# Two-layer hybrid encoder on one core: the end of the expert stage reordered, with the output in four transfers

## The chip, the core and the metric

The kernel runs on one core of a Trainium2 chip. A core has TensorE (PE, matrix products and transposes), VectorE (DVE), ScalarE (ACT), GpSimd (POOL) and SyncE (SP, which here only issues DMAs). Engines run their own instruction streams and meet at semaphores. The metric is the device time of one execution in microseconds (us), lower is better.

## The reference

A sequence of 16 meta tokens and 256 real tokens (width 1024) passes two layers. Each layer has a mixer (three groups of token mixers between one input and one output projection) and a feed-forward part. The second layer's feed-forward part, the one that the change touches, is a mixture of 8 experts of which each token uses 2:

```python
def moe_swiglu(h, router_w, w_gate, w_up, w_down):
    ...
    for e in range(N_EXPERTS):
        out = out + combine[..., e:e + 1].astype(h.dtype) * swiglu(h, w_gate[e], w_up[e], w_down[e])
    return out
```

where `swiglu(h, g, u, d)` is `(silu(h @ g) * (h @ u)) @ d`, the gate and up matrices are 1024 x 3584 and the down matrix is 3584 x 1024. The result is added to `h`, and the meta tokens are dropped: 256 x 1024 floats (1 MB) are the output.

## The kernel before

**The expert stage.** It takes the second half of the execution. For each expert the at most 128 tokens that chose it are gathered into `xe_hi`/`xe_lo`. An expert's 3584 hidden columns are done in 7 chunks of 512; with 8 experts there are 56 chunks, numbered n = 0 to 55 (`LAST` is 55). Every product is made of three passes over a high and a low part of each factor (`three`): high by high, low by high, high by low. If more than 128 tokens chose one expert, a flag `crowd` is set and a second pass (`experts(1)`) is run; each engine reads the flag (`value_load`) and branches around that code.

**Weights.** A chunk has six units of 128 x 2048 floats (1 MB): two for gate, two for up, two for down. `moe_stream` has SP load them into six raw slots in order. ACT makes the high part of unit k (`hi(k)`, L768, tile `m_hi`), DVE the low part (`lo(k)`, L1130, tile `m_lo`), into a ring of four. `hi(k)` waits until PE has used unit k - 3 in full (`m_used >= k - RING + 1`), as both share a slot of the ring. The order of the 336 units puts the down units of chunk n behind the gate and up units of chunk n + 1. For the end this gives: units 328 to 331 are gate and up of chunk 55, 332 and 333 down of chunk 54, 334 and 335 down of chunk 55.

**A chunk on PE** (`experts` of the tensor block): `wide` makes the gate product (bank 0), then the up product (bank 1); ACT takes SiLU (`silu`, tile `eg`), DVE multiplies (`hidden`, L1660, tile `eh`). PE goes on with `tall(n - 1)`, the down product of the chunk before, into banks 3 and 4 (the two halves of the 1024 output columns), and then `turn_hidden(n)` transposes `eh` in four pieces (L2254, bank 2). ACT and DVE make `et_hi` and `et_lo` of it (`et_high` L1005, `et_low` L1664). There is one `et_hi` and one `et_lo`.

**The end of an expert.** When its last chunk's `tall` is done, ACT copies banks 3 and 4 scaled by the gate to `ye_hi` (`ye_high`, L1021, 1024 columns at once), DVE makes `ye_lo` (L1683), PE multiplies by the selection matrix to bring the rows back to their tokens (`scatter`, L2289 and L2290, eight products into four banks), and DVE adds the four banks to `acc` (`add_scattered`, L1695). Within the stage this overlaps the next expert; for the last expert nothing follows.

**The order at the end** is written out by hand. On PE: `tall(54)`, `turn_hidden(55)`, `tall(55)`, `scatter(7)`. On ACT and DVE:

```python
                et_high(pas, LAST)
                hi(pas * MOE_UNITS + MOE_UNITS - 2)
                hi(pas * MOE_UNITS + MOE_UNITS - 1)
                ye_high(pas, NEXP - 1)
...
                hidden(pas, LAST)
                et_low(pas, LAST)
                lo(pas * MOE_UNITS + MOE_UNITS - 2)
                lo(pas * MOE_UNITS + MOE_UNITS - 1)
                ye_low(pas, NEXP - 1)
```

After the four adds DVE reads `crowd`, branches, and does a small memset (L1740) that signals `moe_done`. SP waits for it and sends the whole of `acc` in one DMA (L683), waits until that has landed, and all engines meet at the end of the program (L330).

Of the kernel before, what the change touches and what calls it, by code (L numbers as in the profile page):

```python
# [23 lines left out]
P = 128  # L24
# [49 lines left out]
PAIRS = NEXP // 2  # L74
MOE_UNITS = 6 * CHUNKS * NEXP
RING = 4
UNIT = 2048
PART = UNIT // 2
SPLITS = 4
# [73 lines left out]
def tall_units(n):  # L153

    return chunk_units(n + 1) + 4 if n < CHUNKS * NEXP - 1 else MOE_UNITS - 2
# [171 lines left out]
def program(nc, a, out):  # L327

    ctx = ExitStack()
    with ctx:  # L330
        def sem(name):
            return ctx.enter_context(nc.semaphore(name))
# [143 lines left out]
        x_hi = put("x_hi", [P, 2, D], F32R)  # L476
        x_lo = put("x_lo", [P, 2, D], F32R)
        acc = put("acc", [P, 2, D])
        xe_hi = [put(f"xe_hi{i}", [P, KT, 2 * P], F32R) for i in range(2)]
        xe_lo = [put(f"xe_lo{i}", [P, KT, 2 * P], F32R) for i in range(2)]  # L480
        et_hi = put("et_hi", [P, 4, P], F32R)
# [13 lines left out]
        eh = put("eh", [P, 512])  # L495
        assert mark[0] <= sq_at + 4 * T * 4
        put, mark = region(u32_at)
        ye_hi = put("ye_hi", [P, D], F32R)
        ye_lo = put("ye_lo", [P, D], F32R)
        m_hi_at = (u_at, split_at, split_at + UNIT * 4, h_at)  # L500
# [29 lines left out]
        for l in range(DEPTH):  # L530
# [13 lines left out]
        crowd_ready, moe_done = sem("crowd_ready"), sem("moe_done")  # L544

        mat = lambda n: mats[:, n, :]
        ident = mat(M_ID)
# [79 lines left out]

        mslot = lambda k: (NU + SHIFT + k) % RAW_SLOTS
        LAST = CHUNKS * NEXP - 1


        def gather_step(n):
# [15 lines left out]
        def moe_stream(sp):  # L648

            def experts(pas):  # L650
                for u in range(MOE_UNITS):
                    k = pas * MOE_UNITS + u
                    if k < RAW_SLOTS:
                        sp.wait_ge(lo_ready, 2 * (NU + k - RAW_SLOTS + 1))
                    else:
                        sp.wait_ge(m_lo_ready, k - RAW_SLOTS + 1)
                    sp.dma_start(raw[:, mslot(k), :], a["moe_units"][u]).then_inc(raw_full[mslot(k)], 16)
            experts(0)

            sp.wait_ge(crowd_ready, 1)  # L660
            with sp.If(sp.value_load(crowd[0:1, 0:1], min_val=0, max_val=1) > 0):
                experts(1)


        @block.sync
        def _(sp):
            sp.dma_start(h[:, :, 0:META], a["meta_t"].rearrange("(k p) n -> p k n", p=P)).then_inc(h_in, 16)
            sp.dma_start(h[:, :, META:T], a["x_t"].rearrange("(k p) n -> p k n", p=P)).then_inc(h_in, 16)
            for u, (nk, width, pieces) in enumerate(units):
                if slot_before[u] is not None:  # L670
                    sp.wait_ge(lo_ready, 2 * slot_before[u] + 2)
                for l in range(DEPTH):
                    if u == out_units[l][2]:
                        sp.wait_ge(lo_ready, 2 * out_units[l][0])
                        sp.dma_start(w_uq[:, :, :], a["mla_w_uq"][l].rearrange("(k p) n -> p k n", p=P)).then_inc(mla_w_in, 16)
                        sp.dma_start(w_ukv[:, :], a["mla_w_ukv"][l]).then_inc(mla_w_in, 16)
                        ml[l][2].wait(sp, 0, "o", H * len(QUERIES[l]) - 1)
                v = raw_view(u)
                for c0, src in pieces:
                    sp.dma_start(v[:, :, c0:c0 + src.shape[2]], src).then_inc(raw_full[slot_of[u]], 16)  # L680
            moe_stream(sp)
            sp.wait_ge(moe_done, 1)
            sp.dma_start(out[0].rearrange("(t p) n -> p t n", p=P), acc[:, :, :]).then_inc(out_sent, 16)  # L683
            sp.wait_ge(out_sent, 16)


        @block.gpsimd
# [31 lines left out]
        def _(act):  # L719
# [282 lines left out]

            def et_high(pas, n):
                act.wait_ge(turned, pas * (LAST + 1) + n + 1)
                nc.scalar.activation(et_hi[:, :, :], heads(ps[:, 2, :]), ACT.Copy).then_inc(et_hi_ready, 1)  # L1005

            def xe_copy(pas, p, step, banks):
                act.wait_ge(gathered, 4 * (pas * PAIRS + p) + step + 1)
# [48 lines left out]
        def _(dve):  # L1057
# [603 lines left out]

            def et_low(pas, n):
                dve.wait_ge(et_hi_ready, pas * (LAST + 1) + n + 1)
                V.tensor_tensor(et_lo[:, :, :], heads(ps[:, 2, :]), et_hi[:, :, :].bitcast(F32),  # L1664
                                ALU.subtract).then_inc(et_ready, 1)

            def select(pas, p):
# [11 lines left out]
                V.tensor_copy(gslot[:, p % 2, :], ps[:, GATHER[0], 0:2]).then_inc(gslot_ready, 1)  # L1679

            def ye_low(pas, e):
                dve.wait_ge(ye_hi_ready, pas * NEXP + e + 1)
                V.scalar_tensor_tensor(ye_lo[:, :].rearrange("p (b n) -> p b n", b=2), ps[:, 3:5, :],  # L1683
                                       gslot[:, e // 2 % 2, e % 2:e % 2 + 1],
                                       ye_hi[:, :].bitcast(F32).rearrange("p (b n) -> p b n", b=2),
                                       ALU.mult, ALU.subtract).then_inc(ye_ready, 1)

            def add_scattered(pas, e, i):

                q = (3, 2, 0, 1)[i]  # L1690
                dve.wait_ge(scattered, pas * NEXP + e + 1)
                if pas or e:
                    dve.wait_ge(acc_added, 4 * (pas * NEXP + e))
                part = acc[:, q // 2, 512 * (q % 2):512 * (q % 2) + 512]
                V.tensor_tensor(part, part, ps[:, SCATTER[q], :], ALU.add).then_inc(acc_added, 1)  # L1695

            def experts(pas):
                select(pas, 0)
                for n in range(LAST + 1):
# [37 lines left out]
            dve.wait_ge(crowd_ready, 1)  # L1737
            with dve.If(dve.value_load(crowd[0:1, 0:1], min_val=0, max_val=1) > 0):
                experts(1)
            V.memset(cols[:, 59:60], 0.0).then_inc(moe_done, 1)  # L1740


        @block.tensor
        def _(pe):
# [472 lines left out]
            def views(k, nk):  # L2217
                return tuple(w[k % RING][:, :].rearrange("p (k n) -> p k n", k=nk) for w in (m_hi, m_lo))
# [9 lines left out]
                                     kt == 0, kt == KT - 1)  # L2228
                    last.then_inc(m_used, 1)

            def tall(pas, n):

                pe.wait_ge(et_ready, pas * (LAST + 1) + n + 1)
                c = n % CHUNKS
                for i in range(2):
                    k = pas * MOE_UNITS + tall_units(n) + i
                    pe.wait_ge(m_lo_ready, k + 1)
                    wh, wl = views(k, 2)
                    for j in range(2):
                        f = 2 * i + j  # L2240
                        for b in range(2):
                            cb = slice(512 * b, 512 * b + 512)
                            last = three(ps[:, 3 + b, :], (et_hi[:, f, :], et_lo[:, f, :]), (wh[:, j, cb], wl[:, j, cb]),
                                         c == 0 and f == 0, c == CHUNKS - 1 and f == 3)
                    last.then_inc(m_used, 1)

            def turn_hidden(pas, n):
                pe.wait_ge(eh_ready, pas * (LAST + 1) + n + 1)
# [32 lines left out]
            def scatter(pas, e):  # L2281

                pe.wait_ge(sel_t_ready, pas * PAIRS + e // 2 + 1)
                pe.wait_ge(ye_ready, pas * NEXP + e + 1)
                for t in range(2):
                    for hf in range(2):
                        o = ps[:, SCATTER[2 * t + hf], :]
                        s_t = sel_t[e // 2 % 2][:, e % 2, t, :]
                        mm(o, s_t, ye_hi[:, 512 * hf:512 * hf + 512], start=True, stop=False)  # L2289
                        i = mm(o, s_t, ye_lo[:, 512 * hf:512 * hf + 512], start=False, stop=True)  # L2290
                i.then_inc(scattered, 1)

            def experts(pas):
                if pas:
# [5 lines left out]
                for n in range(LAST + 1):  # L2300
# [60 lines left out]
```

## Time and profile before

| what | value |
|---|---|
| time, median of 3 runs | 2056.36 us (2055.69, 2056.36, 2062.05) |
| the profiled execution's own time | 2062.42 us |
| its span, first to last instruction | 2060.6 us |
| PE busy in the span | 1941.4 us (94%) |
| DVE busy | 1518.7 us (74%) |
| ACT busy | 1122.4 us (54%) |
| mean granted clock of PE | 0.955 of full |
| moved by DMA | 443.59 MB, 215 GB/s on average |

All times within the execution are counted from the span's start. A matrix product's record is longer than the distance to the next one, since products are pipelined: the distance between starts is what one costs, and the record's end is when its result is there. Busy shares are averages over stages with different limits, so the end of the program has to be read by itself.

### The profile page before, as it was taken

The page shows a single profiled execution, that of the slowest core. Times are in us where ns is not written, and L with a number is a line of the kernel's source. Part 1 is how long each engine was busy: PE and PEld are TensorE (multiplying, and loading weights), DVE is VectorE, ACT ScalarE, POOL GpSimd, SP SyncE. Part 2 cuts the span into 40 slices and gives each one's busy share as a digit, 9 for nine tenths or more (in the row PEclk, how much of TensorE's full clock was granted, in tenths as well). Part 3 has the DMA queues.
Part 4 walks back from the last instruction along what each step waited for, and adds up shares of the span by engine and source line. Part 5 has one row for each costly group of instructions (what it writes and reads, how often), then busy time and mean ns, then how long its engine had stood idle before and what let it go on. Part 6 is the DMA issues. An engine that isn't in the chain of part 4 may idle for free.

```text
span 2060.6 us, 26977 instructions
## 1 busy us (share of the span) xinstructions
PE 1941.4 (94%) x10940; PEld 1653.9 (80%) x10940; DVE 1518.7 (74%) x1877; ACT 1122.4 (54%) x1235; POOL 73.7 (4%) x67
## 2 busy tenths in 40 slices
PE   7998989889999987988999999999999999999996
PEld 6986858789998985767878888888888888888885
DVE  6757586555547757675668888988889898888884
ACT  4642242343334542423367777777777777777773
POOL 1001111000000001111000000000000000000000
PEclk9996899999999997989899999999999999999998
DMA  9500000645545500002559999999999999999992
GB/s 300 156 26 1 1 1 1 194 144 172 165 128 169 154 27 0 1 1 82 195 220 355 359 351 352 351 351 354 350 362 351 347 352 356 356 354 365 353 366 89
DMA packets 139122, 443.59 MB, mean 215 GB/s; under 512 B 14320, under 2 KB 94240, under 8 KB 95856
## 3 DMA queue, kind: packets, MB, share of 16 engines
q1 hardware_dynamic: 137968, 437.87, 58.5%
q0 software_dynamic: 1024, 3.93, 0.5%
q8 instruction: 89, 1.46, 0.3%
q14 instruction: 41, 0.34, 0.0%
HBM read 439.61 MB, written 2.16 MB: 214 GB/s over the span
## 4 chain that ended last, share of the span: by engine, by line
PE 86%; DVE 10%; issue 2%; ACT 1%; DMA 0%; POOL 0%; SPq 0%; DVEq 0%; ACTq 0%; POOLq 0%
PE ps L1751 22%; PE ps L1753 22%; PE ps L1752 22%; PE ps L2134 2%; PE ps L2119 2%; PE ps L2138 2%; DVE cacc L1173 2%; PE ps L1764 2%; DVE w_lo L1073 1%; PE ps L1913 1%; PE ps L2254 1%; PE ps L1960 1%; PE ps L2265 1%; PE ps L1996 1%; PE ps L1925 0%
## 5 line engine op out<-in xcount | busy, mean ns | idle before, releaser
L1130 DVE TENSOR_TENSOR m_lo<-raw,m_hi 128x2048 fp32r<-128x2048 f32 x336 | 768.5, 2291 | 145.4 <-ACT m_hi L768 145.4
L768 ACT ACTIVATE m_hi<-raw 128x2048 fp32r<-128x2048 f32 x336 | 644.0, 1918 | 273.2 <-PE ps L1753 273.2
L1751 PE MATMUL ps<-m_hi,xe_hi 128*128 128x512 f32 x896 | 358.5, 400 | 1.1 <-ACT xe_lo L1010 1.1
L1753 PE MATMUL ps<-m_lo,xe_hi 128*128 128x512 f32 x896 | 353.6, 395 | 0.0
L1752 PE MATMUL ps<-m_hi,xe_lo 128*128 128x512 f32 x896 | 353.6, 395 | 0.0
L1073 DVE TENSOR_TENSOR w_lo<-raw,w_hi 128x1024 fp32r<-128x1024 f32 (+1 forms) x164 | 183.5, 1156 | 123.8 <-ACT w_hi L733 123.7
L1751 PE MATMUL ps<-u_hi,w_hi 128*128 128x272 f32 x800 | 238.7, 298 | 15.5 <-DVE u_lo L1123 11.8
L1753 PE MATMUL ps<-u_lo,w_hi 128*128 128x272 f32 x800 | 234.9, 294 | 0.0
L1752 PE MATMUL ps<-u_hi,w_lo 128*128 128x272 f32 x800 | 233.8, 292 | 0.0
L733 ACT ACTIVATE w_hi<-raw 128x1024 fp32r<-128x1024 f32 (+1 forms) x164 | 159.6, 1002 | 124.5 <-PE ps L1753 124.4
L1753 PEld LDWEIGHTS ps<-m_lo,xe_hi 128*128 128x128 f32 x896 | 168.0, 187 | 41.2
L1751 PEld LDWEIGHTS ps<-m_hi,xe_hi 128*128 128x128 f32 x896 | 168.1, 188 | 39.9 <-ACT xe_lo L1010 1.3
L1752 PEld LDWEIGHTS ps<-m_hi,xe_lo 128*128 128x128 f32 x896 | 168.2, 188 | 38.4
L1751 PE MATMUL ps<-m_hi,et_hi 128*128 128x512 f32 x448 | 178.6, 399 | 4.9 <-DVE m_lo L1130 4.9
L1752 PE MATMUL ps<-m_hi,et_lo 128*128 128x512 f32 x448 | 177.9, 397 | 0.0
L1753 PE MATMUL ps<-m_lo,et_hi 128*128 128x512 f32 x448 | 177.7, 397 | 0.0
L1751 PEld LDWEIGHTS ps<-u_hi,w_hi 128*128 128x128 f32 x800 | 154.2, 193 | 20.0 <-issue 19.5
L1752 PEld LDWEIGHTS ps<-u_hi,w_lo 128*128 128x128 f32 x800 | 154.4, 193 | 0.5
L1753 PEld LDWEIGHTS ps<-u_lo,w_hi 128*128 128x128 f32 x800 | 154.0, 193 | 0.0
L1751 PEld LDWEIGHTS ps<-m_hi,et_hi 128*128 128x128 f32 x448 | 84.7, 189 | 25.0 <-issue 5.1
L1753 PEld LDWEIGHTS ps<-m_lo,et_hi 128*128 128x128 f32 x448 | 84.7, 189 | 20.9
L1752 PEld LDWEIGHTS ps<-m_hi,et_lo 128*128 128x128 f32 x448 | 84.7, 189 | 19.9
(373 smaller groups left out, 2770.4 us busy)
## 6 DMA issues: line engine op xcount, KB each, us to landing
raw<-in_moe_units SPq DMA_DIRECT2D x336, 1024.0 KB, 4.9
raw<-in_w_in SPq DMA_DIRECT2D x30, 1024.0 KB, 5.6
raw<-in_w_out SPq DMA_DIRECT2D x16, 768.0 KB, 5.4
raw<-in_ffn_w_gate SPq DMA_DIRECT2D x11, 1024.0 KB, 5.2
raw<-in_ffn_w_up SPq DMA_DIRECT2D x11, 1024.0 KB, 5.4
raw<-in_ffn_w_down SPq DMA_DIRECT2D x8, 896.0 KB, 4.8
raw<-in_ffn_w_down SPq DMA_DIRECT2D x4, 1024.0 KB, 5.2
w_uq<-in_mla_w_uq SPq DMA_DIRECT2D x2, 768.0 KB, 4.3
```

Of the source, the lines that this page charges most:

```text
L733: nc.scalar.activation(w_hi[q % SPLITS][:, 0:r.shape[1]], r, ACT.Copy).then_inc(hi_ready, 1)
L768: nc.scalar.activation(m_hi[k % RING][:, :], raw[:, slot, :], ACT.Copy).then_inc(m_hi_ready, 1)
L1073: V.tensor_tensor(w_lo[q % SPLITS][:, 0:r.shape[1]], r, w_hi[q % SPLITS][:, 0:r.shape[1]].bitcast(F32), ALU.subtract).then_inc(lo_ready, 1)
L1130: V.tensor_tensor(m_lo[k % RING][:, :], raw[:, mslot(k), :], m_hi[k % RING][:, :].bitcast(F32), ALU.subtract).then_inc(m_lo_ready, 1)
L1173: i = V.scalar_tensor_tensor(dst, src, w, dst, ALU.mult, ALU.add)
L1751: mm(o, w[0], x[0], start=first, stop=False)
L1752: mm(o, w[1], x[0], start=False, stop=False)
L1753: return mm(o, w[0], x[1], start=False, stop=last)
L1764: last = mm(ps[:, STAT_BANKS[k % 2], 0:width], mat(which)[0:r], sq[0:r, (piece[0] - 1) % 4, 0:width], start=(i == 0), stop=(i == len(rows) ...
L2119: i = mm(o, B[d]["M"][:, hh, :], B[d]["T"][:, hh, :], start=True, stop=True)
L2134: i = mm(ps[:, 2 * d + 1, hp * hh:hp * hh + hp], B[d]["X"][:, hh, :], level_cols(B[d]["TT"], n, 1 - d, hh), start=True, stop=True)
L2138: i = mm(ps[:, 2 * d + 1, H * hp + hp * hh:H * hp + hp * hh + hp], B[d]["TT"][:, hh, :], level_cols(B[d]["X"], n, d, hh), start=True, stop ...
```

## The change

Only the last chunk and the last expert are handled in another way, and the output is sent in another form.

- ACT: `hi(334)` and `hi(335)` stand ahead of `et_high(55)`. DVE: `lo(334)`, `hidden(55)`, `lo(335)`, `et_low(55)` in this order.
- PE: `tall` does one unit per call. In chunk 55 `turn_hidden(55)` stands between the two units of `tall(54)`. `et_hi`/`et_lo` of chunk 55 are tiles of their own, laid where `xe_hi[0]` was.
- `last_tall`: the same 24 products, but all of bank 3 first, with a signal `first_half`, then all of bank 4.
- `ye_high`, `ye_low` and the scatter of the last expert work on 512 columns at a time, and the two adds of a half follow its scatter.
- SP sends each quarter of `acc` (128 rows x 512 columns, 256 KB) as soon as it is added; `moe_done` and its memset are gone.
- All other chunks keep their order; `tall(n, 1)` repeats the wait on `et_ready`.

```diff
+QUARTERS = ((0, 0), (1, 0), (0, 1), (1, 1))
...
+        et_hi = [et_hi, nc.alloc_sbuf_tensor_at("et_hi_last", [P, 4, P], F32R, offset=xe_at)]
+        et_lo = [et_lo, nc.alloc_sbuf_tensor_at("et_lo_last", [P, 4, P], F32R, offset=xe_at + 4 * P * 4)]
...
-            sp.wait_ge(moe_done, 1)
-            sp.dma_start(out[0].rearrange("(t p) n -> p t n", p=P), acc[:, :, :]).then_inc(out_sent, 16)
-            sp.wait_ge(out_sent, 16)
+            for i, (t, hf) in enumerate(QUARTERS):
+                sp.wait_ge(acc_added, 4 * (NEXP - 1) + i + 1)
+                cs = slice(512 * hf, 512 * hf + 512)
+                sp.dma_start(out[0, P * t:P * t + P, cs], acc[:, t, cs]).then_inc(out_sent, 16)
+            sp.wait_ge(out_sent, 64)
...
+            def last_ye_high(pas, hf):
+                act.wait_ge(*((m_used, (pas + 1) * MOE_UNITS) if hf else (first_half, pas + 1)))
+                nc.scalar.activation(ye_hi[:, 512 * hf:512 * hf + 512], ps[:, 3 + hf, :], ACT.Copy,
+                                     scale=gslot[:, (PAIRS - 1) % 2, 1:2]).then_inc(ye_hi_ready, 1)
...
-                et_high(pas, LAST)
                 hi(pas * MOE_UNITS + MOE_UNITS - 2)
                 hi(pas * MOE_UNITS + MOE_UNITS - 1)
-                ye_high(pas, NEXP - 1)
+                et_high(pas, LAST)
+                act.wait_ge(gslot_ready, (pas + 1) * PAIRS)
+                last_ye_high(pas, 0)
+                last_ye_high(pas, 1)
...
+            def last_ye_low(pas, hf):
+                dve.wait_ge(ye_hi_ready, (pas + 1) * YE - 1 + hf)
+                cs = slice(512 * hf, 512 * hf + 512)
+                V.scalar_tensor_tensor(ye_lo[:, cs], ps[:, 3 + hf, :], gslot[:, (PAIRS - 1) % 2, 1:2], ye_hi[:, cs].bitcast(F32),
+                                       ALU.mult, ALU.subtract).then_inc(ye_ready, 1)
...
+            def add_last(pas):
+
+                dve.wait_ge(acc_added, 4 * (pas * NEXP + NEXP - 1))
+                for i, (t, hf) in enumerate(QUARTERS):
+                    dve.wait_ge(scattered, (pas + 1) * YE - 1 + i // 2)
+                    add_part(t, hf)
...
+                lo(pas * MOE_UNITS + MOE_UNITS - 2)
                 hidden(pas, LAST)
+                lo(pas * MOE_UNITS + MOE_UNITS - 1)
                 et_low(pas, LAST)
-                lo(pas * MOE_UNITS + MOE_UNITS - 2)
-                lo(pas * MOE_UNITS + MOE_UNITS - 1)
-                ye_low(pas, NEXP - 1)
-                for i in range(4):
-                    add_scattered(pas, NEXP - 1, i)
+                last_ye_low(pas, 0)
+                last_ye_low(pas, 1)
+                add_last(pas)
...
-            V.memset(cols[:, 59:60], 0.0).then_inc(moe_done, 1)
...
+            def last_tall(pas):
+
+                pe.wait_ge(et_ready, (pas + 1) * (LAST + 1))
+                k = pas * MOE_UNITS + MOE_UNITS - 2
+                pe.wait_ge(m_lo_ready, k + 2)
+                for b in range(2):
+                    cb = slice(512 * b, 512 * b + 512)
+                    for f in range(4):
+                        wh, wl = views(k + f // 2, 2)
+                        last = three(ps[:, 3 + b, :], (et_hi[1][:, f, :], et_lo[1][:, f, :]),
+                                     (wh[:, f % 2, cb], wl[:, f % 2, cb]), False, f == 3)
+                    if b == 0:
+                        last.then_inc(first_half, 1)
+                last.then_inc(m_used, 2)
...
+            def last_scatter(pas):
+
+                for hf in range(2):
+                    pe.wait_ge(ye_ready, (pas + 1) * YE - 1 + hf)
+                    cs = slice(512 * hf, 512 * hf + 512)
+                    for t in range(2):
+                        o = ps[:, SCATTER[2 * t + hf], :]
+                        s_t = sel_t[(PAIRS - 1) % 2][:, 1, t, :]
+                        mm(o, s_t, ye_hi[:, cs], start=True, stop=False)
+                        i = mm(o, s_t, ye_lo[:, cs], start=False, stop=True)
+                    i.then_inc(scattered, 1)
...
                     if n:
-                        tall(pas, n - 1)
+                        tall(pas, n - 1, 0)
+                    if n and n < LAST:
+                        tall(pas, n - 1, 1)
                     turn_hidden(pas, n)
-                tall(pas, LAST)
-                scatter(pas, NEXP - 1)
+                tall(pas, LAST - 1, 1)
+                last_tall(pas)
+                last_scatter(pas)
```

## Rows read from the trace of the kernel before

**Rows 1.** The page: its span, and the chain that ended last, by engine.
```profile
span 2060.6 us, 26977 instructions
...
PE 86%; DVE 10%; issue 2%; ACT 1%; DMA 0%; POOL 0%; SPq 0%; DVEq 0%; ACTq 0%; POOLq 0%
```

**Rows 2.** Stretch: length, PE, PEld, DVE, ACT, POOL busy (count), clock, DMA share, GB/s.
```profile
1997.00:2015.00 18.00, 18.00 (x81) 14.45 (x80) 15.26 (x9) 12.80 (x9) 0.00 (x0) 1.00 0.97 368
```

**Rows 3.** Timeline of PE, last full chunk: start us, us, engine, line, operation.
```profile
2023.81 0.39 PE L1753 MATMUL ps<-m_lo,xe_hi 128*128 128x512 f32 x1
...
2026.61 0.39 PE L1753 MATMUL ps<-m_lo,xe_hi 128*128 128x512 f32 x1
2026.84 0.39 PE L1751 MATMUL ps<-m_hi,et_hi 128*128 128x512 f32 x1
...
2032.44 0.60 PE L2254 MATMUL ps<-mats,eh 128*128 128x128 f32 x4
```

**Rows 4.** Timeline of ACT, the end; in brackets idle time before and its releaser.
```profile
2018.70 1.92 ACT L768 ACTIVATE m_hi<-raw 128x2048 fp32r<-128x2048 f32 x1 [0.84 <-PE ps L1753]
...
2023.32 0.57 ACT L1001 ACTIVATE eg<-ps 128x512 f32<-128x512 f32 x1
2033.07 0.60 ACT L1005 ACTIVATE et_hi<-ps 128x512 fp32r<-128x512 f32 x1 [9.18 <-PE ps L2254]
2033.57 3.70 ACT L768 ACTIVATE m_hi<-raw 128x2048 fp32r<-128x2048 f32 x2
2046.13 1.11 ACT L1021 ACTIVATE ye_hi<-ps,gslot 128x1024 fp32r<-128x1024 f32 x1 [8.86 <-PE ps L1753]
```

**Rows 5.** Timeline of DVE, the end.
```profile
2027.09 0.69 DVE L1660 TENSOR_TENSOR eh<-eg,ps 128x512 f32<-128x512 f32 x1 [1.36 <-PE ps L1753]
2033.70 0.69 DVE L1664 TENSOR_TENSOR et_lo<-ps,et_hi 128x512 fp32r<-128x512 f32 x1 [5.92 <-ACT et_hi L1005]
2035.50 4.49 DVE L1130 TENSOR_TENSOR m_lo<-raw,m_hi 128x2048 fp32r<-128x2048 f32 x2 [1.11 <-ACT m_hi L768]
2047.27 1.28 DVE L1683 SCALAR_TENSOR_TENSOR ye_lo<-ps,gslot,ye_hi 128x1024 fp32r<-128x1024 f32 x1 [7.28 <-ACT ye_hi L1021]
2051.53 2.48 DVE L1695 TENSOR_TENSOR acc<-acc,ps 128x512 f32<-128x512 f32 x4 [2.97 <-PE ps L2290]
2055.86 0.06 DVE L1740 MEMSET cols<- 128x1 f32 x1 [1.84 <-issue]
```

**Rows 6.** Timeline of PE, the last chunk's down product and the scatter.
```profile
2037.94 0.77 PE L1751 MATMUL ps<-m_hi,et_hi 128*128 128x512 f32 x1 [4.90 <-DVE m_lo L1130]
...
2045.69 0.40 PE L1753 MATMUL ps<-m_lo,et_hi 128*128 128x512 f32 x1
...
2048.70 0.47 PE L2289 MATMUL ps<-ye_hi,sel_t 128*128 128x512 f32 x1 [2.61 <-DVE ye_lo L1683]
...
2050.86 0.63 PE L2290 MATMUL ps<-ye_lo,sel_t 128*128 128x512 f32 x1
```

**Rows 7.** Busy time and granted clock in short stretches (columns as in rows 2).
```profile
2036.00:2037.00 1.00, 0.00 (x0) 0.00 (x0) 1.00 (x1) 1.00 (x1) 0.00 (x0) 0.60 0.00 0
...
2043.00:2044.00 1.00, 1.00 (x5) 0.83 (x5) 0.00 (x0) 0.00 (x0) 0.00 (x0) 0.98 0.00 0
...
2049.80:2050.20 0.40, 0.40 (x3) 0.29 (x2) 0.00 (x0) 0.00 (x0) 0.00 (x0) 0.57 0.08 21
```

**Rows 8.** DVE's instructions of the line that branches on `crowd`: duration ns, start.
```profile
L1738 DVEq COMPARE_BRANCH  x1: 72/72/72, 2052.8 to 2052.8; - x1
```

**Rows 9.** DMA issues: out<-in, queue, count, KB each, median us from issue to landing.
```profile
raw<-in_moe_units SPq DMA_DIRECT2D x336, 1024.0 KB, 4.9
...
out_h<-acc SPq DMA_DIRECT2D x1, 1024.0 KB, 4.3
...
h<-in_meta_t SPq DMA_DIRECT2D x1, 64.0 KB, 2.5
```

**Rows 10.** Timeline of SP, its last issue.
```profile
2055.94 0.40 SPq L683 DMA_DIRECT2D out_h<-acc  x1
```

More of the change, by code:

```diff
@@ L478, in program @@
         acc = put("acc", [P, 2, D])
+        xe_at = mark[0]
         xe_hi = [put(f"xe_hi{i}", [P, KT, 2 * P], F32R) for i in range(2)]
@@ L543, in program @@
             "ye_hi_ready", "ye_ready", "scattered", "acc_added"))
-        crowd_ready, moe_done = sem("crowd_ready"), sem("moe_done")
+        first_half = sem("first_half")
+        crowd_ready = sem("crowd_ready")
         mat = lambda n: mats[:, n, :]
@@ L629, in program @@
         LAST = CHUNKS * NEXP - 1
+        YE = NEXP + 1
         def gather_step(n):
@@ L662, in moe_stream @@
                 experts(1)
+                sp.wait_ge(acc_added, 8 * NEXP)
         @block.sync
@@ L1004, in et_high @@
                 act.wait_ge(turned, pas * (LAST + 1) + n + 1)
-                nc.scalar.activation(et_hi[:, :, :], heads(ps[:, 2, :]), ACT.Copy).then_inc(et_hi_ready, 1)
+                nc.scalar.activation(et_hi[n == LAST][:, :, :], heads(ps[:, 2, :]), ACT.Copy).then_inc(et_hi_ready, 1)
             def xe_copy(pas, p, step, banks):
@@ L1663, in et_low @@
                 dve.wait_ge(et_hi_ready, pas * (LAST + 1) + n + 1)
-                V.tensor_tensor(et_lo[:, :, :], heads(ps[:, 2, :]), et_hi[:, :, :].bitcast(F32),
+                V.tensor_tensor(et_lo[n == LAST][:, :, :], heads(ps[:, 2, :]), et_hi[n == LAST][:, :, :].bitcast(F32),
                                 ALU.subtract).then_inc(et_ready, 1)
@@ L1681, in ye_low @@
             def ye_low(pas, e):
-                dve.wait_ge(ye_hi_ready, pas * NEXP + e + 1)
+                dve.wait_ge(ye_hi_ready, pas * YE + e + 1)
                 V.scalar_tensor_tensor(ye_lo[:, :].rearrange("p (b n) -> p b n", b=2), ps[:, 3:5, :],
@@ L1686, in ye_low, with add_part @@
                                        ALU.mult, ALU.subtract).then_inc(ye_ready, 1)
+            def last_ye_low(pas, hf):
[3 more added lines that the diff above has]
+                                       ALU.mult, ALU.subtract).then_inc(ye_ready, 1)
+            def add_part(t, hf):
+                part = acc[:, t, 512 * hf:512 * hf + 512]
+                V.tensor_tensor(part, part, ps[:, SCATTER[2 * t + hf], :], ALU.add).then_inc(acc_added, 1)
             def add_scattered(pas, e, i):
-                q = (3, 2, 0, 1)[i]
-                dve.wait_ge(scattered, pas * NEXP + e + 1)
+                dve.wait_ge(scattered, pas * YE + e + 1)
                 if pas or e:
                     dve.wait_ge(acc_added, 4 * (pas * NEXP + e))
-                part = acc[:, q // 2, 512 * (q % 2):512 * (q % 2) + 512]
-                V.tensor_tensor(part, part, ps[:, SCATTER[q], :], ALU.add).then_inc(acc_added, 1)
+                add_part(*((1, 1), (1, 0), (0, 0), (0, 1))[i])
+            def add_last(pas):
[3 more added lines that the diff above has]
+                    add_part(t, hf)
             def experts(pas):
@@ L2229, in wide, with tall @@
                     last.then_inc(m_used, 1)
-            def tall(pas, n):
+            def tall(pas, n, i):
                 pe.wait_ge(et_ready, pas * (LAST + 1) + n + 1)
                 c = n % CHUNKS
[L2235 to L2245, printed above, removed]
+                k = pas * MOE_UNITS + tall_units(n) + i
+                pe.wait_ge(m_lo_ready, k + 1)
+                wh, wl = views(k, 2)
+                for j in range(2):
+                    f = 2 * i + j
+                    for b in range(2):
+                        cb = slice(512 * b, 512 * b + 512)
+                        last = three(ps[:, 3 + b, :], (et_hi[0][:, f, :], et_lo[0][:, f, :]), (wh[:, j, cb], wl[:, j, cb]),
+                                     c == 0 and f == 0, c == CHUNKS - 1 and f == 3)
+                last.then_inc(m_used, 1)
+            def last_tall(pas):
+                pe.wait_ge(et_ready, (pas + 1) * (LAST + 1))
+                k = pas * MOE_UNITS + MOE_UNITS - 2
+                pe.wait_ge(m_lo_ready, k + 2)
+                for b in range(2):
+                    cb = slice(512 * b, 512 * b + 512)
+                    for f in range(4):
[5 more added lines that the diff above has]
+                last.then_inc(m_used, 2)
             def turn_hidden(pas, n):
@@ L2283, in scatter @@
                 pe.wait_ge(sel_t_ready, pas * PAIRS + e // 2 + 1)
-                pe.wait_ge(ye_ready, pas * NEXP + e + 1)
+                pe.wait_ge(ye_ready, pas * YE + e + 1)
                 for t in range(2):
```

## Prediction

> **What bounds the kernel now.** The chain that ended last lies on PE for 86% of the span [rows 1], and within the expert stage on nothing else: in a stretch of 18 us near its end PE is busy for all of it at full clock, DVE 15.26 us, ACT 12.80 us [rows 2]. DMA has a share of 0.97 there, but SP is held back by raw slots that DVE frees, so the stream follows PE. A chunk is 72 products at 0.233 us (the twelve from the start at 2023.81 to that at 2026.61 took 2.80 us [rows 3]) and four transposes, 17.2 us. The change leaves that as it is. What it edits begins at 2032.4, so I read the timelines from there on as a list of who waits.
>
> PE ends `tall(54)`, transposes `eh` at 2032.44 [rows 3], and then has nothing: ACT makes `et_hi` at 2033.07 and only then `m_hi` of units 334 and 335 (3.70 us) [rows 4], DVE `et_lo` and then both `m_lo`, from 2035.50 for 4.49 us [rows 5]. PE starts on the first of them at 2037.94, idle for 4.90 us [rows 6]. In that gap its granted clock falls from 1.00 to half (mean 0.60 in the slice where it falls), and it is back only at 2043.0 [rows 7], so that the 24 products of the last `tall` take 8.16 us (2037.94 to the record end at 2046.10) instead of 5.8. Then the end of an expert runs bare: `ye_hi` 1.11 us, `ye_lo` 1.28, eight products from 2048.70 to 2051.49, the last ones again at half clock [rows 4 to 7], four adds of 2.48 us ending at 2054.01, DVE's branch and the memset at 2055.86 [rows 5], the issue at 2055.94 [rows 10], the landing 4.3 us later [rows 9], and 0.36 us to the end.
>
> **The early splits.** `hi(334)` needs unit 330 used. ACT and DVE start 0.5 us behind the start of the product that they wait for (`eh` at 2027.09 for 2026.61 [rows 3, 5]), so it starts at 2023.81 + 0.50 = 2024.3; ACT is free by then, its last work being SiLU at 2023.32 for 0.57 us. At 1.92 us [rows 4] it ends at 2026.2. `hi(335)` starts at 2026.61 + 0.50 = 2027.1 and ends at 2029.0. Both units have landed long before. The load of 335 waits for the low part of unit 329, three units ahead of the `hi(332)` at 2018.70, so `hi(329)` is at about 2018.7 - 3 x 2.8 - 0.4 = 2009.9 (with the four transposes between), its low part done 4.2 us later at 2014.1, and the load landed 4.9 us after that [rows 4, 9], at about 2019, an estimate. DVE: `lo(334)` 2026.2 to 2028.5. `hidden(55)` now stands behind it and starts at 2028.5 instead of 2027.09; what waits for it is only `turn_hidden(55)`. It ends at 2029.15. `lo(335)` 2029.1 to 2031.4.
>
> **PE.** `tall(54, 0)` runs 2026.84 to 2029.64 (12 x 0.2333). `eh` is there with 0.49 us to spare, the thinnest margin of the change; each us beyond it would be a us of PE. Transposes to 2030.1, `tall(54, 1)` to 2032.89. Under it ACT makes `et_hi` (record end of the transposes 2030.24, 0.60 us, to 2030.9) and DVE `et_lo` behind `lo(335)`, 2031.3 to 2032.0: 0.9 us to spare. The second price of an early `et_hi` would be the one tile still read by `tall(54, 1)`; the tiles of its own remove it. So `last_tall` starts at 2032.89 without a gap. There has been no idle time for the clock to fall in, and 24 products at 0.233 us end at 2038.65, its last start being 2038.26 and a record 0.39 us. Against 2046.10 that is **7.45 us** less: 5.05 of wait, 2.4 of clock.
>
> **The last expert.** Bank 3 is complete at 2035.85; its `ye_hi`, `ye_lo` hide under the other bank's 2.8 us. On the path stands the second half alone. A half `ye_hi` is costed by `et_hi`, the same engine and 512 columns (0.60, against 1.11 + 0.02 gap; saves **0.53**); a half `ye_lo` by `et_lo` (0.69 against 1.28; saves **0.59**). Scatter products of the first half fill PE from 2038.5 to 2039.4, under the split of the second. The second half's four start 0.13 us behind `ye_lo` as before, at 2040.1, and end at 2041.3 at full clock: 1.18 us against 2.81, **1.63** less. DVE adds the first half as soon as it is through with `ye_lo` (2039.9, two at 0.60 us apart), done by the time the second comes. Then two adds take 1.28 us instead of 2.48, **1.20** less, and end at 2042.6. SP waits on the adds themselves, so from 2054.01 to 2055.94, 1.93 us, only 0.03 remain: **1.90** less. The sum so far is 13.3 us: the last issue at 2042.6.
>
> **The output.** The last transfer has 256 KB. The trace has 4.3 us for 1 MB and 2.5 us for 64 KB [rows 9]; on the line between them 256 KB take 2.5 + 1.8 x 192/960 = 2.9 us, an estimate. The bounds are 2.5 and 4.3. I take 2.9, **1.4** less. The four issues are 0.6 to 0.7 us apart or more, and an issue is 0.40 us [rows 10], so SP keeps up. Landing 2045.5, end about 2045.9.
> The Trainium skill, "DMA: Bandwidth & Descriptors", section "Anatomy of one DMA", gives about 2.0 us plus bytes over 436 GB/s for GpSimd's path. For 1 MB that is an estimated 4.4 us, and this trace agrees with 4.3 for SP's. For 256 KB it is 2.6, which would make the sum 0.3 us larger.
>
> **A floor below it.** After its last add DVE still branches, and the jump past the second pass takes from 2052.8 to 2055.86 [rows 5, 8], 4.35 us counted from the end of the last scatter product. Nobody waits for it but the end of the program: 2041.3 + 4.35 = 2045.65, just what the landing gives. So a quicker landing would gain nothing, and the other cover is thin too: the end is at 2045.9 to 2046.1.
>
> **Sum.** 13.3 + 1.4 = 14.7, less 0.1 for that tie: span 2060.6 - 14.6 = 2046.0. The profiled execution took 2062.42 us, 6.06 more than the median of the runs, so the forecast is made from the median: 2056.36 - 14.6 = 2041.8 us, 0.7% less. The clock's share (2.4 here and 0.8 in the scatter) is the part that may differ among executions; all have the 4.90 us gap before.
>
> **The rivals.**
> *A, as above,* with its own range: landing at 4.3 instead of 2.9 (1.3 less gain), margins missed by half a us each, clock at half in the last four products (4 x 0.19 = 0.8): gain 12 to 15, so 2041 to 2044.5 before the spread of runs.
> *B, the clock falls nevertheless,* within `last_tall`, for instance since it falls late (in the scatter it fell at 2049.8, while PE was busy again for a us [rows 7]). A product then costs 0.427 instead of 0.233: 28 x 0.194 = 5.4 us back, 2047.2. Against it: where PE has no gap the clock is 1.00 [rows 2], and `last_tall` follows such a stretch without one.
> *C, four transfers cost more than one.* If they ran one behind another at 4.3 us each from the first issue at 2040.6, the last would land at 2057.8: gain 2.4, 2054.0, no change to be seen. Against it: the weights' units take 4.9 us each to land [rows 9] and come every 2.9 us, so transfers overlap. The milder form is the landing's bound in A.
> The Trainium skill, same page, section "Bandwidth", says to batch DMAs to 1 MB or more. As far as that concerns throughput it has no object in 1 MB of output; whether it hurts is C.
> *D, the stall stays.* One of the chains in front of `last_tall` is late (ACT or DVE held by an order that I misread) and PE idles as before, with its clock. Then 7.45 us are lost of the gain: 7.2 remain, 2049.2, at the edge of what can be told.
> *E, slower.* `tall(n, 1)` waits once more on `et_ready` in chunks 0 to 53, on the engine that bounds the stage. The gain is used up at 14.6/54 = 0.27 us each, more than a product; from 0.39 us on it is slower by 0.3% (2063). Against it: between 2026.61 and 2026.84, where PE passes the waits on `et_ready` and `m_lo_ready`, products are 0.23 us apart as elsewhere [rows 3], so a satisfied wait costs nothing visible.
>
> **Numbers.** A 0.76, B 0.06, C 0.05 (with a mild form that still gains), D 0.06, E 0.03, and 0.04 for shifts of the first thousand us that have nothing to do with this. About 0.3% (6.2 us) is what a measurement of this kernel tells from no change; the three runs of before lie 6.4 us apart. Faster: A and B, most of C's mild form, half of D: 0.92. Same 0.05, slower 0.03. The range takes A with the spread of a median upward (the runs scatter 0.7 down and 5.7 up) and B: 2039.0 to 2047.5.
>
> **What would show it.** Right: no idle time of PE between 2024 and 2038.5; the last transposes at about 2029.6, with products of `tall(54)` before and behind them; granted clock 1.00 until 2038; `m_hi` x2 before `et_hi` on ACT; `eh` at 2028.5; last add ending at 2042.6; last output issue there and landing in 2.5 to 3.2 us. Wrong: an idle gap in front of the transposes (margin 0.49 gone), a clock below 1.00 in `last_tall`, chunks longer than 17.24 us, or an end set by DVE's jump well past the landing.

## The result and the profile after

The changed kernel takes 2046.61 us (median of 6 runs, 2043.37 to 2047.77) beside 2057.12 us of the kernel before (6 runs, 2055.11 to 2062.05). The ratio is 0.9936, 95% interval 0.9923 to 0.9949: by it the kernel is 13.2 us faster, 10.5 to 15.8, while the two medians alone lie 10.5 us apart. Forecast were a gain of 14.6 us and a time of 2041.8 us. The time is 4.8 us above the forecast and within its range of 2039.0 to 2047.5; the gain forecast is within the interval.

The profiled execution has a span of 2046.0 us, the very number of the forecast, and that is luck: the change brought 0.95 us less than the sum said, and the part ahead of it happened to be 0.95 us shorter. Everything ahead of the change ran 0.95 us earlier in this execution than in the one of before: the first product of `tall(54)` starts at 2025.89 instead of 2026.84. From here on all tails are counted from that product to the end of the span: 33.76 us before, 20.11 after, a gain of **13.65 us** where the sum said 14.6.

ACT after the change, timeline of the end (columns as in rows 4; lines have moved):

```profile
2026.15 1.92 ACT L777 ACTIVATE m_hi<-raw 128x2048 fp32r<-128x2048 f32 x1 [0.88 <-PE ps L1783]
2029.33 0.60 ACT L1014 ACTIVATE et_hi_last<-ps 128x512 fp32r<-128x512 f32 x1 [1.26 <-PE ps L2298]
...
2037.73 0.69 ACT L1035 ACTIVATE ye_hi<-ps,gslot 128x512 fp32r<-128x512 f32 x1 [2.05 <-PE ps L1783]
```

DVE, the same:

```profile
2027.51 0.68 DVE L1676 TENSOR_TENSOR eh<-eg,ps 128x512 f32<-128x512 f32 x1
2028.11 2.29 DVE L1146 TENSOR_TENSOR m_lo<-raw,m_hi 128x2048 fp32r<-128x2048 f32 x1
2030.31 0.68 DVE L1680 TENSOR_TENSOR et_lo_last<-ps,et_hi_last 128x512 fp32r<-128x512 f32 x1
...
2038.45 0.75 DVE L1707 SCALAR_TENSOR_TENSOR ye_lo<-ps,gslot,ye_hi 128x512 fp32r<-128x512 f32 x1 [1.99 <-ACT ye_hi L1035]
2039.12 2.64 DVE L1712 TENSOR_TENSOR acc<-acc,ps 128x512 f32<-128x512 f32 x4
```

PE, the same (the transposes, the first product behind them, the first and last of `last_tall`, the second half's scatter):

```profile
2025.89 0.39 PE L1781 MATMUL ps<-m_hi,et_hi 128*128 128x512 f32 x1
...
2028.69 0.60 PE L2298 MATMUL ps<-mats,eh 128*128 128x128 f32 x4
2029.05 0.48 PE L1781 MATMUL ps<-m_hi,et_hi 128*128 128x512 f32 x1
...
2031.93 0.39 PE L1781 MATMUL ps<-m_hi,et_hi_last 128*128 128x512 f32 x1
...
2037.30 0.40 PE L1783 MATMUL ps<-m_lo,et_hi_last 128*128 128x512 f32 x1
...
2039.26 0.50 PE L2345 MATMUL ps<-ye_hi,sel_t 128*128 128x512 f32 x1 [0.63 <-DVE ye_lo L1707]
```

The low part of unit 335 is made by 2030.4 instead of 2040.0 [rows 5]. The transposes stand 2.80 us behind the first product of `tall(54)`, with no idle time before them. PE then goes through to the end of `last_tall` with nothing in brackets, at full clock, as two stretches of it show (columns as in rows 2):

```profile
2034.00:2036.00 2.00, 2.00 (x10) 1.59 (x9) 0.29 (x1) 0.69 (x1) 0.00 (x0) 1.00 0.00 0
2036.00:2038.00 2.00, 2.00 (x11) 1.59 (x9) 0.46 (x1) 0.27 (x1) 0.00 (x0) 1.00 0.00 0
```

The one surprise stands at the output. SP's first and last issue, each from its own stretch of the timeline, the landing times of the four, and the last instructions of DVE and SP (ns min/median/max, start):

```profile
2039.83 0.35 SPq L692 DMA_DIRECT2D out_h<-acc  x1
```
```profile
2041.79 1.47 SPq L692 DMA_DIRECT2D out_h<-acc  x1
```
```profile
DMA to landing us min/median/max: 2.2/3.1/3.8
```
```profile
L331 DVEq DRAIN  x1: 58/58/58, 2044.8 to 2044.8; - x1
...
L331 SPq DRAIN  x1: 7/7/7, 2045.8 to 2045.8; - x1
```

The last issue starts 0.03 us behind the last add, as forecast, but takes 1.47 us where the first takes 0.35, and its data land 3.8 us later. DVE is through with its jump at 2044.8, before SP.

The jumps themselves, PE's and then DVE's branch on the flag (ns min/median/max, start):

```profile
L2395 PEldq COMPARE_BRANCH  x1: 4010/4010/4010, 2040.2 to 2040.2; - x1
```
```profile
L1769 DVEq COMPARE_BRANCH  x1: 72/72/72, 2041.7 to 2041.7; - x1
```

PE's branch is under way for 4.01 us, from 2040.22 to 2044.23, and so during the last three issues. DVE's record is short, but its next instruction comes 3.1 us behind it.

### The profile page after: what moved, and what is told of

Read it like the earlier page. It is cut to its first block, busy times and chain, and to the rows that moved or that the text cites. A ratio compares the mean times of both kernels' runs of the same rounds, so it can differ in the third digit from the quotient of the medians.

```text
span 2046.0 us, 27032 instructions
## 1 busy us (share of the span) xinstructions
PE 1941.8 (95%) x10940; PEld 1654.7 (81%) x10940; DVE 1516.8 (74%) x1877; ACT 1122.4 (55%) x1236; POOL 73.9 (4%) x67
## 3 DMA queue, kind: packets, MB, share of 16 engines
q8 instruction: 90, 1.47, 0.3%
## 4 chain that ended last, share of the span: by engine, by line
PE 87%; DVE 9%; issue 1%; DMA 1%; ACT 1%; POOL 0%; DVEq 0%; POOLq 0%; ACTq 0%
PE ps L1781 22%; PE ps L1783 22%; PE ps L1782 22%; PE ps L2164 2%; PE ps L2149 2%; PE ps L2168 2%; PE ps L1794 2%; DVE cacc L1189 2%; DVE w_lo L1089 1%; PE ps L1943 1%; PE ps L2298 1%; PE ps L1990 1%; PE ps L2309 1%; PE ps L1806 1%; PE ps L2026 1%
## 5 line engine op out<-in xcount | busy, mean ns | idle before, releaser
L1781 PE MATMUL ps<-m_hi,et_hi 128*128 128x512 f32 x440 | 174.4, 396 | 0.0
L1782 PE MATMUL ps<-m_hi,et_lo 128*128 128x512 f32 x440 | 173.8, 395 | 0.0
```

The lines of the kernel that those rows point to most:

```text
L1781: mm(o, w[0], x[0], start=first, stop=False)
L1782: mm(o, w[1], x[0], start=False, stop=False)
```

## The experiments

**Late splits.** Is the largest term, 7.45 us, a wait and a clock that fell in it?

```diff
-                hi(pas * MOE_UNITS + MOE_UNITS - 2)
-                hi(pas * MOE_UNITS + MOE_UNITS - 1)
                 et_high(pas, LAST)
+                hi(pas * MOE_UNITS + MOE_UNITS - 2)
+                hi(pas * MOE_UNITS + MOE_UNITS - 1)
...
-                lo(pas * MOE_UNITS + MOE_UNITS - 2)
                 hidden(pas, LAST)
-                lo(pas * MOE_UNITS + MOE_UNITS - 1)
                 et_low(pas, LAST)
+                lo(pas * MOE_UNITS + MOE_UNITS - 2)
+                lo(pas * MOE_UNITS + MOE_UNITS - 1)
```

> The changed kernel with the split order of before on ACT and DVE (et_high(55) first, hidden and et_low(55) first, then units 334 and 335); all else as changed. All tails are measured from the first product of tall(54) to the end of the span: 33.8 us before, 20.1 us after. Theory (the 7.45 us were a wait and a clock that fell in it): PE idles some 4.5 us in front of last_tall, the granted clock falls to half in the gap, and some 10 to 12 products cost 0.43 us, 2.0 to 2.4 us in all: tail 27 us. Rival (the wait alone mattered, the clock would have been the same): 24.6 us. Rival (the early splits were not what took the wait away): 20.1 us.

Measured: tail 27.05 us. Timed against the kernel before the ratio is 0.9961 (0.9946 to 0.9975): all parts but the early splits are worth 0.4%, about 8 us of a time near 2060 (5 to 11), beside 6.7 us by the tails. PE before the last chunk's products, and the clock ahead of them and over the first twelve of them:

```profile
2036.96 0.76 PE L1781 MATMUL ps<-m_hi,et_hi_last 128*128 128x512 f32 x1 [4.31 <-DVE m_lo L1146]
```
```profile
2034.00:2035.00 1.00, 0.00 (x0) 0.00 (x0) 1.00 (x2) 0.08 (x1) 0.00 (x0) 1.00 0.00 0
```
```profile
2036.96:2042.10 5.14, 5.14 (x12) 4.08 (x13) 0.00 (x0) 0.00 (x0) 0.00 (x0) 0.50 0.01 3
```

The wait is back, and twelve products at half clock take 5.14 us. The clock fell within the gap: its mean is 0.82 from 2035.5 to 2036 and 0.50 from there on. Both parts are as expected; the second rival (early splits without effect) is out.

**Late splits, filled.** The same, with PE kept busy in the wait.

```diff
                 tall(pas, LAST - 1, 1)
+                for _ in range(18):
+                    mm(ps[:, 0, :], x_hi[:, 0, 0:P], x_lo[:, 0, 0:512], start=True, stop=True)
                 last_tall(pas)
```

> As the run with late splits, with 18 products of 512 columns (one low part by one high part of the tokens, results unused) put on PE between tall(54) and last_tall, to keep PE busy in the wait. If idleness lets the clock fall, the clock stays at 1.00, last_tall's 24 products take 5.8 us, and the tail is 24.6 us, 2.0 to 2.4 us below the unfilled one. If the clock falls for another reason, 27 us as without.

Measured: tail 24.56 us, 2.49 below the unfilled one; the clock over the last chunk's products stays full:

```profile
2035.80:2041.70 5.90, 5.85 (x25) 4.81 (x26) 0.75 (x1) 0.69 (x1) 0.00 (x0) 1.00 0.00 0
```

So the two parts of the first term come apart: 24.56 - 20.11 = 4.45 us of wait and 2.49 us of clock, which fell because PE was idle. Useless work in the gap gave a third of the term back. The two add up to 6.94 us and not to 7.45, since the gap of these kernels is 4.31 us and that of the kernel before was 4.90 [rows 6]. All further kernels were timed once, so from here on the tails of the traces are compared, not the times.

**Whole last expert.** What are the halves worth?

```diff
                 for f in range(4):
                     wh, wl = views(k + f // 2, 2)
                     for b in range(2):
...
-                last_ye_high(pas, 0)
-                last_ye_high(pas, 1)
+                act.wait_ge(m_used, (pas + 1) * MOE_UNITS)
+                nc.scalar.activation(ye_hi[:, :].rearrange("p (b n) -> p b n", b=2), ps[:, 3:5, :], ACT.Copy,
+                                     scale=gslot[:, (PAIRS - 1) % 2, 1:2]).then_inc(ye_hi_ready, 2)
```

(and `ye_low` and the scatter likewise.)

> The changed kernel without the halves: last_tall goes through both banks per 128 rows as tall does, the last ye_hi and ye_lo are 1024 columns at once, the scatter is eight products with one signal, and the four adds follow; early splits and four output transfers stay. From the profile of the changed kernel the halves were worth 0.42 (ye_hi), 0.62 (ye_lo), 1.61 (scatter) and 1.20 (adds), 3.85 us: tail 24.0 us. If the clock also falls while PE waits 2.6 us for ye_lo, 0.8 us more, 24.8 us. Rival (the halves gain nothing, since the end is set by DVE's jump past the second pass or by the output): 20 to 21 us.

Measured: tail 23.70 us, 3.59 above the changed kernel's. The clock did not fall in the wait for `ye_lo`, though it is longer; the second row is the stretch of the eight products (columns as in rows 2):

```profile
2041.07 0.50 PE L2347 MATMUL ps<-ye_hi,sel_t 128*128 128x512 f32 x1 [2.67 <-DVE ye_lo L1765]
```
```profile
2041.07:2043.19 2.12, 2.11 (x8) 1.42 (x8) 0.00 (x0) 0.00 (x0) 0.00 (x0) 1.00 0.05 12
```

The eight products take 2.12 us, against 2.79 in the kernel before, when the clock fell within them. So 3.85 us was too much for the halves by themselves: its 1.61 us for the scatter held that fall. The last issue begins 19.20 us into the tail, against 15.90 in the changed kernel: up to there the halves are worth 3.30 us. The other 0.3 us are the output's, whose issues and landings in this run are (durations in ns, then us to landing):

```profile
L692 SPq DMA_DIRECT2D out_h<-acc x4: 332/338/351, 2044.0 to 2045.8; - x4
```
```profile
DMA to landing us min/median/max: 2.4/2.7/4.1
```

All four issues are short, against 1.47 us for the changed kernel's fourth, at the same distance of 0.6 us and with the same three transfers under way. That speaks against a limit on transfers under way. But the fourth lands 4.1 us after its issue, later than any quarter of the changed kernel, so a late landing does not need a slow issue.

**One, two, three transfers, and two queues.** Where did the output's gain go? The four forms differ from the changed kernel in SP's part alone (and ACT's in the last), for instance for one transfer:

```diff
-            for i, (t, hf) in enumerate(QUARTERS):
-                sp.wait_ge(acc_added, 4 * (NEXP - 1) + i + 1)
...
+            sp.wait_ge(acc_added, 4 * NEXP)
+            sp.dma_start(out[0].rearrange("(t p) n -> p t n", p=P), acc[:, :, :]).then_inc(out_sent, 16)
+            sp.wait_ge(out_sent, 16)
```

> The changed kernel with one output transfer of 1 MB behind the fourth add, straight on the semaphore of the adds. By the prediction's line between 64 KB and 1 MB the quarter transfers gained 1.4 us, less 0.1: tail (from the first product of tall(54) to the end) 20.1 + 1.3 = 21.4 us. By the changed kernel's profile, in which the last quarter took 3.8 us to land with an issue of 1.47 us: the whole lands 4.3 us after its issue, tail 20.6 us, issue 0.40 us.

> The changed kernel with two transfers of 512 KB, one for each half, behind the second and fourth add. Theory (a fourth transfer is issued slowly while three are under way in SP's queue): both issues take 0.33 to 0.40 us, the last lands in about 3.3 us, tail 19.6 us. Rival (SP's last issue is slow whatever stands before it, for instance since its code has to be fetched): last issue above 1 us, tail 20.6 us or more.

> The changed kernel with three transfers: the first half in one (512 KB), then the two last quarters. Theory (number under way): third issue 0.33 to 0.40 us, lands in 2.6 to 2.9 us; then DVE's jump (its end at 18.9 us into the tail) stands at the end: tail 19.2 us. Rival (bytes under way limit the issue, or the last issue is always slow): last issue above 1 us and a tail of 20 us as with four.

> The changed kernel with quarters 1 and 3 issued by SP and quarters 2 and 4 by ACT, which is idle. If the slow fourth issue comes from what SP's own queue has under way, all four issues take 0.33 to 0.40 us (ACT's perhaps somewhat more), the last lands in 2.5 to 3 us, and DVE's jump ends the program: tail 19.2 us. If the limit is shared by the queues, the fourth is slow on ACT too and the tail stays at 20 us.

| output in | issues, us (shortest / longest) | landing, us (shortest / longest) | tail, us |
|---|---|---|---|
| one of 1 MB | 0.40 | 4.7 | 21.05 |
| two of 512 KB | 0.39 / 0.40 | 4.0 / 4.7 | 20.96 |
| 512 KB and two of 256 KB | 0.35 / 1.41 | 3.3 / 4.3 | 20.62 |
| four of 256 KB (the change) | 0.33 / 1.47 | 2.2 / 3.8 | 20.11 |
| four, two of them from ACT | 0.34 / 2.52 | 2.3 / 4.3 | 22.29 |

Neither the number of transfers under way nor "the last issue is always slow" explains this. A third transfer is issued as slowly as a fourth, so it is not the count. A second is issued fast and then lands in 4.7 us, as long as 1 MB, so it is not the issue alone, and not the size either. The one large transfer itself lands 0.4 us later than in the kernel before (4.3 [rows 9]), where it was issued after DVE's jump. ACT as a second issuer makes it worse, being slow in its first issue. What all share is that the output is now sent while PE and DVE jump past the second pass. The DMA queues of the changed kernel from 2039.8 to 2044.5 say what else is on the DMA engines (queue, packets, MB, share):

```profile
q1 hardware_dynamic: 562, 1.03, 59.7%
q8 instruction: 1, 0.02, 1.7%
q14 instruction: 2, 0.02, 1.4%
```

**No second pass; the jumps moved.** So the next kernels take the jumps away from the output:

```diff
+            dve.wait_ge(out_sent, 64)
             dve.wait_ge(crowd_ready, 1)
             with dve.If(dve.value_load(crowd[0:1, 0:1], min_val=0, max_val=1) > 0):
```

(This is DVE's part; `pe` has the same line instead or as well, by run. In these kernels a second pass could not run, and a wait of SP within it is out. In the first of them, `experts(1)` and its branches are out on every engine.)

> The changed kernel with the second pass and its branches left out on all engines (the case that more than 128 tokens choose one expert is then not computed; these inputs don't have it). Theory (SP's slow fourth issue and the late landings come from the code that DVE and PE fetch at their jumps while the output is sent): no code fetch beside the output, four issues of 0.33 to 0.36 us, the last lands in 2.4 to 2.9 us, and nothing else stands at the end: tail 18.7 to 19.2 us against 20.1. Rival (three transfers of 256 KB under way hold up the fourth issue): fourth issue 1.3 us or more, tail 19.9 to 20.2 us.

> The changed kernel in which DVE and PE wait for the output to have landed before they read the flag and jump, with all the code left in (a second pass could not run in this form). It keeps the program's size and moves the two fetches behind the output. Theory: four issues of 0.33 to 0.36 us and a last landing of 2.4 to 2.9 us, at 18.5 to 18.8 us of the tail, and then the jump of some 4 us in the open: tail 22.5 to 23.5 us. Rival (transfers under way): fourth issue 1.3 us or more, last landing 3.6 to 3.8 us.

> The changed kernel in which DVE alone waits for the output to have landed before it reads the flag and jumps (a second pass could not run in this form); PE jumps as in the changed kernel. If DVE's jump is what slows SP's fourth issue: four issues of 0.33 to 0.36 us, last landing 2.1 to 2.9 us after its issue. If PE's is: a slow issue of 1 us or more stays. If each adds a share: an issue between. The tail, 22.5 to 23.7 us, is set by DVE's late jump and says nothing.

> As the last one with PE alone waiting for the output, DVE jumping as in the changed kernel. If DVE's jump is what slows the fourth issue: 1.3 to 1.5 us as in the changed kernel, last landing 3.4 to 3.8 us. If PE's is: four short issues, last landing 2.1 to 2.9 us. The tail is set by PE's late jump.

| jumps during the output | longest issue, us | landing, us (shortest / median / longest) | tail, us |
|---|---|---|---|
| PE's and DVE's (the change) | 1.47 | 2.2 / 3.1 / 3.8 | 20.11 |
| none, no second pass | 0.35 | 2.0 / 2.1 / 2.2 | 18.41 |
| none, both behind the output | 0.35 | 2.1 / 2.5 / 2.7 | 23.69 |
| PE's only | 1.37 | 2.1 / 3.1 / 3.7 | 23.65 |
| DVE's only | 0.35 | 2.1 / 2.6 / 2.9 | 23.57 |

The two rows with neither jump still differ, 2.2 and 2.7 us for the longest landing; in the second ACT still branches, ahead of its output, and the code is all there. Which of the two it is stays open.

The slow issue comes with PE's jump: of this table it is there in both kernels that have that jump during the output and in none of the three that do not. Issue durations in ns (min/median/max) of the kernel with PE's jump alone during the output, and with DVE's alone:

```profile
L691 SPq DMA_DIRECT2D out_h<-acc x4: 332/347/1369, 2040.7 to 2042.7; - x4
```
```profile
L691 SPq DMA_DIRECT2D out_h<-acc x4: 332/338/352, 2042.0 to 2043.9; - x4
```

With it goes a fetch of code on queue q8. The queues for the same two, from 2040.6 to 2046.8 and from 2041.9 to 2047.2 (first output issue to SP's end):

```profile
q8 instruction: 2, 0.03, 2.2%
q14 instruction: 1, 0.01, 0.7%
```
```profile
q1 hardware_dynamic: 576, 1.05, 53.9%
q14 instruction: 2, 0.02, 1.4%
```

The Trainium skill, "Advanced Engine Details and Errata", section "ISA Cache", has code cached in lines of 16 KB. The two q8 packets of 0.03 MB together agree with that size; the two of q14, 0.02 MB together, are half as large. The kernel without the second pass has no packet of either queue beside its output.

The kept traces say when the q8 packet moves. In every kernel that keeps the second pass the first one starts 1.0 to 1.7 us behind the start of PE's branch, also where that branch stands behind the output, so it is PE's. In the changed kernel it is this one, in the stretch from 2041.6 to 2041.7; 79.9% of 16 engines for 0.1 us are 1.28 us of packet time:

```profile
q8 instruction: 1, 0.02, 79.9%
```

The slow issue starts 0.14 us behind it and ends 0.33 us behind its end. It is the same in all six kernels whose SP has a slow issue (the change, both with late splits, three transfers, PE's jump alone, the flag read early): the issue starts 0.05 to 0.49 us after a q8 packet of 0.96 to 1.60 us has started, and ends 0.30 to 0.43 us after that packet's end, about the 0.35 us of an undisturbed issue. So the issue looks held up until the fetch is through. In the whole last expert the packet was over (2044.44) before the fourth issue (2045.80), and in the one transfer the issue began just ahead of it. But two short issues also started while the packet was moving: the second of the two transfers, 0.52 us into one of 1.86 us, and the first of the whole last expert, 0.93 us into one of 1.36 us. Overlap by itself is thus not enough. What else it takes, and why the last landing of the whole last expert is late, stays open. No run moved the fetch without moving PE's branch.

**Flag read early.** A try at a better version that keeps the second pass:

```diff
+            dve.wait_ge(crowd_ready, 1)
+            crowded = dve.value_load(crowd[0:1, 0:1], min_val=0, max_val=1)
             experts(0)
...
-            with dve.If(dve.value_load(crowd[0:1, 0:1], min_val=0, max_val=1) > 0):
+            with dve.If(crowded > 0):
```

(ACT and PE likewise.)

> The changed kernel in which DVE, PE and ACT read the flag into a register ahead of the first expert, so that only the branch is left at the end. DVE's branch comes some 0.9 us earlier, at 14.9 us of the tail, and its end at 18.0 us. If the fetch then collides with the third issue instead of the fourth, that one is slow (1 us or more) and the fourth begins behind it: tail 19.3 to 20.0 us. If the fetch has passed before, four short issues and 19.2 us. If the number of transfers under way is the cause: 20.1 us as before.

Measured: tail 21.16 us, worse by 1.05. The jumps came earlier and met the second transfer instead of the last: that issue took 1.46 us, the following ones queued behind it, and the last began 0.9 us behind its add. An earlier fetch is not a smaller one. Its time of 2044.21 us is the lowest of the kernels run once, for a reason far from the change: its first product of `tall(54)` was at 2021.24, 4.65 us earlier than in the changed kernel. The tail is the measure here, not the time of one run.

## Why the prediction was right, point by point

Distances are from the first product of `tall(54)` in both traces.

| term | forecast gain, us | measured gain, us |
|---|---|---|
| to the end of the last `tall` | 7.45 | 19.26 - 11.81 = 7.45 |
| `ye_hi` | 0.53 | 1.17 - 0.75 = 0.42 |
| `ye_lo` | 0.59 | 1.43 - 0.81 = 0.62 |
| scatter | 1.63 | 2.83 - 1.22 = 1.61 |
| adds | 1.20 | 2.48 - 1.28 = 1.20 |
| add to issue | 1.90 | 1.93 - 0.03 = 1.90 |
| issue to the end | 1.3 (1.4 less the tie) | 4.66 - 4.21 = 0.45 |

**The splits and PE** went as traced from the unit order. `hi(334)` waits for unit 330, four units back in the ring of four, as the prediction has it; "unit k - 3" in the section on the kernel before is one unit off. The thin margin of 0.49 us ahead of the transposes held: no idle time there. The term's two parts, wait and clock, were separated by the filled run.

**The halves.** `ye_hi` on 512 columns took 0.69 us, not the 0.60 of `et_hi`, `ye_lo` 0.75, not the 0.69 of `et_lo`: operations that also read the gate's column are not priced by their plain neighbours. It made the gain of `ye_hi` 0.11 us smaller than forecast, while that of `ye_lo` came out 0.03 larger. The clock stayed full in the scatter as forecast (1.00 from 2039 to 2041).

**The output** is the term that was mis-sized. "256 KB take 2.5 + 1.8 x 192/960 = 2.9 us" and "the four issues are 0.6 to 0.7 us apart or more, and an issue is 0.40 us, so SP keeps up": without the second pass a quarter lands in 2.0 to 2.2 us, below the lower bound of 2.5, and SP does keep up; beside PE's jump the last issue is 1.47 us and its landing 3.8. Two errors of opposite sign, net 0.85 us; that they partly cancelled is luck. The prediction did not mention PE's jump at all. It named DVE's jump as a floor (4.35 us behind the last scatter product, and DVE did end at 2044.8, 2040.44 + 4.36), as work beside the transfer that touches nothing of it. That SP's issues are not all 0.4 us long was in the trace of before: its longest took 6386 ns, in the first 20 us.

The Trainium skill, "DMA: Bandwidth & Descriptors", section "Anatomy of one DMA", would by its figures for GpSimd's path have a quarter take an estimated 2.6 us; the run without the second pass has 2.0 to 2.2 from SP's queue. The rule of its section "Bandwidth", to batch DMAs to 1 MB or more, is given for the share of peak bandwidth. For the end of this kernel the measurement decides the other way: one transfer has the tail 0.94 us longer than four. Its issue starts as soon behind the last add as the fourth quarter's, but 1 MB then lands in 4.7 us and the last quarter in 3.8.

**The rivals.** B (clock falls anyway) is out by the rows of 1.00 in `last_tall`. C (transfers one behind another): what cost there is comes from elsewhere, 18.41 us with four transfers and no jumps. D (the stall stays) is what the late splits look like, 27.05 us, and did not happen. E (waits of the split `tall`): from the first to the last `tall` the 54 chunks take 2026.84 - 1067.16 = 959.68 us before and 2025.89 - 1066.22 = 959.67 after, so 54 further satisfied waits cost nothing that can be seen.

By the time of whole runs the gain of 13.2 us (10.5 to 15.8) can't tell 13.65 from 14.6; the tails of single traces can, since in all eleven kernels that keep the early splits the last `tall` ended 11.80 or 11.81 us into the tail.

## What to carry to other kernels

Where the end of a kernel runs bare, work that depends only on loads (here the splits of the last weights) should be done before the engine that waits has its last dependent step; trace the order of each engine's queue by hand and note each margin. Idle time on PE can be paid twice, once as a wait and once in clock: here the clock cost 2.49 us beside 4.45 us of wait. It need not be: behind a gap of 2.67 us the clock was full. When a gain moves the output earlier, ask what else now runs at the same time: here PE's branch past a large body of code fetched 16 KB at the moment of the last issue.

## What the runs showed of the hardware

- A jump of PE past the second pass, during four output transfers, goes with one SP issue of 1.28 to 1.47 us instead of 0.33 to 0.35 and a last landing of 3.6 to 4.0 us; with DVE's jump alone the issues stay at 0.35 and the last landing is 2.9, with both jumps behind the output 2.7, without the second pass 2.1. Where PE's branch began 2.0 us ahead of the first issue, all issues were short and the last landing was 4.1.
- PE's branch past the second pass is 3.5 to 4.3 us long in the traces, and a code packet of 16 KB on q8 follows its start by 1.0 to 1.7 us. A slow SP issue ended 0.30 to 0.43 us behind that packet's end in six of six cases.
- The granted clock fell in an idle gap of 4.31 us, before the next product, and stayed at half (1.2 of 2.4 GHz) for twelve products, 5.14 us; with the gap filled it stayed at full. After idle gaps of 0.63 us and of 2.67 us the products that followed ran at full clock in these traces, while in the kernel before it fell 1.1 us into the products behind a gap of 2.61 us.
- A write of 256 KB to HBM lands 2.0 to 2.2 us after its issue on SP where no code fetch stands beside it (the kernel without the second pass), with four of them 0.6 to 0.8 us apart.
